# The first unit of two MLPs, multiplied token tile by token tile

## The reference

```python
y = mixer(h)                                     # ... @ w_out
x = layer_norm(DN_ALPHA * x + gate * y, ln_g[layer, 0], ln_b[layer, 0])
shift, scale, gate = ada_modulation(c, ada_w[layer, 1], ada_b[layer, 1])
h = x * (1.0 + scale) + shift
y = jnp.square(jax.nn.relu(h @ w1)) @ w2         # w1 1024 x 4096, w2 4096 x 1024
```

## Time and profile before

| what | value |
|---|---|
| median of 3 runs | 1386.22 us |
| the profiled execution | 1384.38 us |
| its span | 1382.6 us |
| PE busy | 1318.2 us, 95% |
| PE weight loads (PEld) busy | 1118.4 us, 81% |
| DVE busy | 999.9 us, 72% |
| ACT busy | 592.8 us, 43% |
| mean granted clock of PE | 0.994 of full |

### The profile page before, as it was taken

How to read it: one execution, slowest core, us unless ns; L and a number is a source line. 1 busy time by engine, 2 the same in 40 slices (tenths; PEclk the granted TensorE clock), 3 DMA queues, 4 the chain that set the end, 5 groups by cost and what they waited for, 6 DMA issues and landing times.

```text
span 1382.6 us, 21002 instructions
## 1 busy us (share of the span) xinstructions
PE 1318.2 (95%) x8064; PEld 1118.4 (81%) x8064; DVE 999.9 (72%) x1351; ACT 592.8 (43%) x802; POOL 20.2 (1%) x26
## 2 busy tenths in 40 slices
PE   5997999999999999999999999999999989999997
PEld 1844788888788788888899998888888877888886
DVE  3868499888878778766787877666678664566665
ACT  2544344334345543334364334433447553444332
POOL 0000000000000000000000000000000000000000
PEclk9999999999999999999999999999999999999999
DMA  9945458787286437666445313555543332455540
GB/s 363 366 174 216 167 200 320 260 314 268 82 328 221 139 113 290 227 216 223 170 148 204 109 55 127 216 201 189 193 169 124 121 122 80 176 196 202 183 152 31
DMA packets 45953, 264.46 MB, mean 191 GB/s; under 512 B 5432, under 2 KB 7096, under 8 KB 20155
## 3 DMA queue, kind: packets, MB, share of 16 engines
q1 hardware_dynamic: 32784, 218.45, 43.6%
q10 hardware_dynamic: 13102, 45.09, 9.3%
HBM read 260.89 MB, written 1.05 MB: 189 GB/s over the span
## 4 chain that ended last, share of the span: by engine, by line
PE 79%; DVE 11%; DMA 3%; ACT 3%; issue 2%; SPq 1%; POOL 0%; DVEq 0%; POOLq 0%; ACTq 0%
PE banks L611 16%; PE banks L613 15%; PE banks L612 15%; PE banks L976 15%; PE banks L979 7%; DMA A<-ada_w 3%; PE banks L1291 2%; DVE w_lo L1940 2%; PE banks L803 1%; DVE hT L1916 1%; PE banks L926 1%; PE banks L1152 1%; DVE mx L2048 1%; PE banks L856 1%; ACT w_hi L1342 1%
## 5 line engine op out<-in xcount | busy, mean ns | idle before, releaser
L1940 DVE TENSOR_TENSOR w_lo<-raw,w_hi 128x2048 fp32r<-128x2048 f32 x191 | 435.1, 2287 | 104.8 <-ACT w_hi L1342 104.6
L1342 ACT ACTIVATE w_hi<-raw 128x2048 fp32r<-128x2048 f32 x191 | 364.8, 1914 | 224.8 <-PE banks L613 203.3
L976 PE MATMUL banks<-hT,w_hi 128*128 128x512 f32 x896 | 280.8, 395 | 0.0
L611 PE MATMUL banks<-w_hi,R 128*128 128x512 f32 (+1 forms) x624 | 245.1, 393 | 1.3 <-DVE R L1983 1.2
L612 PE MATMUL banks<-w_lo,R 128*128 128x512 f32 (+1 forms) x624 | 241.8, 388 | 0.0
L613 PE MATMUL banks<-w_hi,R 128*128 128x512 f32 (+1 forms) x624 | 241.7, 387 | 0.0
L979 PEld LDWEIGHTS banks<-hT,w_lo 128*128 128x128 f32 x896 | 168.3, 188 | 39.2
L979 PE MATMUL banks<-hT,w_lo 128*128 128x256 f32 x896 | 176.0, 278 | 0.0
L611 PE MATMUL banks<-hT,w_hi 128*128 128x256 f32 x520 | 151.7, 292 | 6.0 <-DVE hT L2400 2.8
L613 PE MATMUL banks<-hT,w_lo 128*128 128x256 f32 x520 | 147.1, 283 | 0.0
L612 PE MATMUL banks<-hT,w_hi 128*128 128x256 f32 x520 | 147.0, 283 | 0.0
(11 more groups left out here) (271 smaller groups left out, 1520.2 us busy)
## 6 DMA issues: line engine op xcount, KB each, us to landing
raw<-stream SPq DMA_DIRECT2D x193, 1024.0 KB, 4.9
A<-ada_w ACTq DMA_DIRECT2D x73, 512.0 KB, 5.6
A<-ada_w SPq DMA_DIRECT2D x5, 1024.0 KB, 18.6
raw<-ada_w SPq DMA_DIRECT2D x3, 1024.0 KB, 9.0
X<-ada_w SPq DMA_DIRECT2D x2, 1024.0 KB, 5.0
A<-ln_g ACTq DMA_DIRECT2D x4, 512.0 KB, 3.7
A<-ln_b ACTq DMA_DIRECT2D x4, 512.0 KB, 5.9
A<-ada_w SPq DMA_DIRECT2D x1, 1536.0 KB
```

The costliest lines, as they stand in the source:

```text
L611: pe.matmul(o, lh, rh, start=start, stop=False, skip_group_check=True)
L976: pe.matmul(two(B[2 * kp + a]), wh[:, kt, P * a:P * a + P], hT[:, :, kt, :], start=kt == 0, stop=False, skip_group_check=True)
L1342: act.activation(w_hi[:, s, :], raw[:, s, :], ACT.Copy).then_inc(hi_done, 1)
L1940: v.tensor_tensor(w_lo[:, s, :], raw[:, s, :], w_hi[:, s, :], ALU.subtract).then_inc(lo_done, 1)
```

## The change

Bounds 0 and 2 and unit 0 of the MLPs m = 0 and 1:

- Unit 0 is multiplied for one token tile at a time: 128 columns per matmul instead of 256, 96 matmuls instead of 48. Twelve of tile 0 (a = 0, kt 0 to 3) come in front of `groups(1)`, the other 36 of tile 0 behind it, and the 48 of tile 1 in `mlp`.
- `claim(n["fill"] % 2)` and the wait for the unit's weights now stand in front of `groups(1)`; the six dummy matmuls behind it are gone.
- VectorE splits tile 0 half 1 in front of `stage` instead of behind it.
- The dummies behind `groups(0)` go from 12 to 9 at bound 0 and from 4 to 8 at bound 2; those within `columns(3)` from 8 to 4.

```diff
+            def up_tile(u0, t, order):
+                u, b = T_unit(u0, 0), n["fill"] % 2
+                wh, wl = parts_of(u, KT)
+                for a, kt in order:
+                    at = 256 * a + P * t
+                    m = mm3(B[b][:, at:at + P], wh[:, kt, P * a:P * a + P], wl[:, kt, P * a:P * a + P],
+                            hT_hi[:, kt, P * t:P * t + P], hT_lo[:, kt, P * t:P * t + P], (t, a, kt) == (0, 0, 0), kt == KT - 1)
+                return m
+
+            def lead_up(u0):
+                claim(n["fill"] % 2)
+                weights(T_unit(u0, 0))
+                pe.wait_ge(pair_ready, n["pair"] - 1)
+                up_tile(u0, 0, [(0, kt) for kt in range(4)])
+                groups(1)
+                up_tile(u0, 0, [(1, kt) for kt in range(4)])
+                pe.wait_ge(pair_ready, n["pair"] - 2)
+                up_tile(u0, 0, [(a, kt) for a in range(2) for kt in range(4, 8)])
...
-                            pe.wait_ge(pair_ready, n["pair"] - (0 if kt or m == 2 else 2 if m < 2 else 1))
+                            pe.wait_ge(pair_ready, n["pair"] - (0 if kt or m == 2 else 1))
...
-                for k in range(2):
+                if m < 2:
+                    pe.wait_ge(pair_ready, n["pair"] - 1)
+                    up_tile(u0, 1, [(a, kt) for a in range(2) for kt in range(4)])
+                    pe.wait_ge(pair_ready, n["pair"])
+                    up_tile(u0, 1, [(a, kt) for a in range(2) for kt in range(4, 8)]).then_inc(unit_done, 1)
+                for k in range(1 if m < 2 else 0, 2):
                     up(k, k, T_unit(u0, k), T_unit(u0, k) % SLOTS)
...
-                    if s_ == 3 and j % 2:
+                    if s_ == 3 and j % 4 == 3:
                         idle(2, 1)
...
-                            idle(2, {0: 12, 2: 4, 3: 11}[b])
+                            idle(2, {0: 9, 2: 8, 3: 11}[b])
                         if units:
                             lead(units)
                         else:
-                            groups(1)
-                            claim(n["fill"] % 2)
-                            idle(n["fill"] % 2, 6)
+                            lead_up({0: M0, 2: M1}[b])
...
                         if b != 1:
-                            n["pair"] += 1
+                            split_part(0, 1)
                         stage(last=False)
-                        if b != 1:
-                            n["pair"] -= 2
-                            split_part(0, 1)
-                            n["pair"] += 1
                         split_part(1, 1)
```

## The result

| what | before | after |
|---|---|---|
| median of 20 executions each (three of the 20 before are those ahead of the prediction) | 1391.43 us | 1394.17 us |
| ratio, with its 95% interval | | 1.0031 [1.0018, 1.0044] |
| the profiled execution | 1384.38 us | 1394.5 us |
| its span | 1382.6 us | 1392.7 us |
| mean granted clock of PE in it | 0.994 | 0.985 |

By the ratio the change makes the kernel slower by 0.31%, 4.3 us on a median of 1391.43 (2.5 to 6.1). The forecast was +4.7. The medians alone are 2.7 us apart.

A forecast was written before the change was run, and what follows sets the result against it. PE was taken to bound the kernel, working without a gap behind both bounds, so unit 1's start decides. +1.6 and +3.1 make +4.7 us, on the median 1386.22 giving 1390.9 us; range 1384.0 to 1393.2.

The forecast's parts named there:

- The price p: Unit 0 at both bounds: each 128-column matmul costs 0.116 us (0.112 to 0.120), limited by loading 128 weight columns.
- A: Unit 0, both bounds: the load hides, narrow matmuls cost half, 0.060 us; 5.3 us faster, 1380.9; chance 0.10.
- B: Unit 0, both bounds: a narrow matmul costs about 0.081 us; 2.0 us faster, 1384.2; chance 0.10.
- D: Unit 0, both bounds: narrow matmuls run at the plain float32 rate, 0.223 us; +25.2 us, 1411.4; chance 0.06.
- Bound 0: First edited place: unit 1 starts at 174.83 + 96p = 185.97 instead of 184.39 us, +1.6 (+1.2 to +2.0).
- The split order, "costs nothing": Bound 0: VectorE's sooner split of tile 0 half 1 hides nothing and costs nothing; no quarter is late: 0.
- Bound 2: Second edited place: unit 1 starts at 508.61 + 96p = 519.75 instead of 516.64 us, +3.1 (+2.7 to +3.5).
- the 0.9 of the four dummies: Bound 2: four dummies fewer within `columns(3)` bring the chain of scale, shift and ScalarE 0.9 us forward.
- The claim as the step that holds everything: Bound 2: twelve matmuls, tile 1's transposes and all behind queue on the claim, held by ScalarE until 507.59 us.
- rival C: Bound 2: with fewer dummies the clock falls to 0.50, adding 0.5 to 1.7 us, 1391.4 to 1392.6; chance 0.09.
- Nothing absorbs the delay: Behind both bounds PE is full, so no delay hides; VectorE and ScalarE get first input later, not more work.
- The sum: Both bounds together: +1.6 + 3.1 = +4.7 us, zero where 192p = 17.59, at p = 0.092; forecast chance 0.65.

The follow-up runs named there:

- the run without a fall: Changed kernel, but at bound 2 tile 1's transposes precede the claim and four dummies, not eight, follow tile 0's; 15.13 us from tile 0's transposes to unit 1.
- the mixed kernel with four dummies fewer: Kernel before, with unit 0 cut to 128 columns only where PE waits, the rest 256, and four dummies fewer in `columns(3)`; 0.9966, median 1386.21 us against 1391.01.

## Why the prediction was right, and where it was wrong

**The price p** was taken as 0.116 from 0.112 to 0.120; it is 0.112, the spacing of loads in the earlier trace rows. Rivals A, B and D fall with it. The rule on the back-to-back issue gap in the Trainium skill, TensorE: Matmul & The Clock Gate (about 81 ns), does not hold for these float32 weights: the traces have 0.112 with 128, 64 and 1 moving columns.

**Bound 0** was forecast as +1.6 (1.2 to 2.0) and is +1.09. The start of the first narrow matmul, 3.70 behind the transposes by the working, was 3.69. The term that was too large is 96p: 96 x 0.004 = 0.4 us, and the turn of tile 1 with its switches 0.1. (The lower end of the forecast range of the sum, 3.8, is 192 x 0.112 - 17.59 = 3.9 by its own terms.) No quarter was late, as worked out, and the nine dummies hid in the wait.

**The split order, "costs nothing"**: in the changed kernel no quarter was late; the changed kernel with the old order was not run. Alone it gains 0.4 at bound 0, because unit 0 then no longer waits at kt 4; I had not looked for that wait in the kernel before.

**Bound 2** was forecast as +3.1 and is +4.3 in the profile. Its terms: the 0.9 of the four dummies is shown by the run without a fall (4.46 instead of 5.36), but with the falls it was not kept: 22.18 in the mean of three profiles with four dummies, 21.88 in the one with eight. The claim as the step that holds everything is shown by the same run without a fall: its first narrow matmul waits 0.74 us for ScalarE, and with the transposes in front of the claim unit 1 comes 15.13 behind the transposes of tile 0. Without a fall the sum is +2.6 (from that run and the 0.82, worked out; the changed kernel itself was never seen without a fall there), 0.5 below the forecast by p. On top comes the clock: 4.26 - 2.6 = 1.6, inside the +0.5 to +1.7 of rival C.

**Rival C** was right in its price; its cause, the removed dummies, does not explain that the clock falls at all. The fall comes with eight dummies too: of nine profiles with eight in `columns(3)`, two had no fall at bound 2, five one of 3.4 us and two one of 6.8. Of eight profiles with four (the one with 64 columns left aside), one had none, one 3.4 us and six 6.8.

**Nothing absorbs the delay**, as forecast: behind bound 2 the rest is +0.27, and all profiles have it within 865.5 to 867.9. But the term 0 for the stage between the bounds ("get their first input later, not more work") was too small. The +0.60 of the two profiles is less than this stage differs by in one kernel (313.36 to 316.17 in three profiles of the one before); at equal time at 0.50 in it, it is some +1.6, a wait of PE for VectorE for the most part, of open cause.

**The sum** was +4.7, and the ratio says +4.3 (2.5 to 6.1). The stages without falls make 1.1 + 2.6 = 3.7. With the falls as seen, bound 2 takes 22.18 us in the mean of three profiles (22.07, 22.54, 21.92) and 18.31 in the mean of the six whose bound 2 is that of before (17.81 twice, 18.55 to 18.57 four times): 3.9, and with 1.1 of bound 0 5.0. Both lie inside the interval. That +4.7 came so near is partly luck: both bounds were forecast 0.5 too high, and the falls at bound 2 (1.3 by these means) and the 1.6 behind bound 0 were not in it.

**The failed step** is "The median before, 1386.22, lies 1.8 above the profiled one; on it the forecast is 1390.9 us", with the range built on it. Both the three executions and the profile were taken as the level of the kernel. Its usual level is a median near 1391 in four of five timings and 1388.41 in the fifth, over 104 executions a mean span of 1388.3, with 10.5 us between the lowest and the highest (1384.55 and 1395.01); the three lay within 1.0 us of each other, and that said nothing of this spread. The profile alone could not have told: its clock of 0.994 turned out to be the upper end of what 104 executions show (0.980 to 0.994). The base was 5.2 too low (1391.43 - 1386.22), and the medians, 2.7 apart instead of 4.7, took 2.0 of that back. 1391.43 + 4.7 would have been 1396.1, and with the measured terms 1391.4 + 3.7 = 1395.1, against 1394.17. My range took in the rivals' costs and no spread of the level.

**What stays open.** Why the clock between the opening and bound 0 falls in its patterns, and what starts one. There the time follows the clock in the profiles (PE busy 6.4 us more at 0.93); for the whole it is a correlation over executions, and the one attempt to move the clock on purpose, in the opening, where PE waits for loads, gained nothing. The groups of runs ran on different chips and at different times, and what of the level belongs to the chip was not separated. Whether four dummies instead of eight make the falls at bound 2 longer: the counts lean that way, and the times of the run with that edit alone do not. What makes VectorE later in the mixer behind a changed bound 0. Where the mixed kernel with four dummies fewer gains what its stages do not show.

## What to carry to other kernels

Splitting a matmul's moving operand is free only down to the width at which the load of its weights is the limit: work it out from the spacing of loads, here 0.112 us for 128 float32 columns against 0.120 for 256 moving ones, so that two narrow matmuls cost 0.224 in place of 0.120. Split only so many matmuls as a gap needs: bound 0 became 0.9 us shorter with 48 narrow ones and 24 wide, and 1.1 longer with 96 narrow. (With that and four dummies fewer the kernel was 0.34% faster, not all of it from there.) An instruction moved in front of a wait costs what is queued behind it, so independent transposes go in front of a claim, not behind it (some 0.85 us here, worked out from one execution). Before a forecast of a few us is put on a base, ask how many executions the base has and how much of it ran at 0.50: a difference can be right to half a microsecond and the time still wrong by the spread of the level. And look at the stages behind the edit in more than one profile of each kernel: here a stage that nobody edited was some 1.6 us longer in the mean.

## What the runs showed of the hardware

- Matmuls with 128 float32 weight columns start every 0.112 us at 2.4 GHz with 128 and with 64 moving columns, and every 0.213 us at 1.2 GHz (64 columns); the load record goes from 0.19 to 0.33 us. The load slows with the granted clock.
- A stream of matmuls with 64 moving columns, PE and PEld busy 5.00 of 5.00 us, was followed by 34.1 us at a granted clock of 0.50, beginning 7.2 us behind its first; the 9.4 us of 84 matmuls with 128 columns, in the changed kernel, were not.
- Dummies that hide in a wait at full clock can outlast it at 0.50: 16 records took 2.17 x 16/18 = 1.9 us at 1.00 and 3.52 at 0.50.
- Executions of one and the same kernel, the one before, differ by 10 us of 1388, and the mean granted clock, 0.980 to 0.994, goes with it: 0.24 us for each us at 0.50.
- In a stretch of 136.12 us, 818 matmul records kept PE busy 121.81 us at a mean clock of 0.99, and 819 kept it busy 128.19 us at 0.93; the stretch became 5.0 us longer.
